# Projecting the two channel tiles of one ring piece back to back in a two-block transformer kernel

## The reference

```python
# block one, last part: 32 experts, each token uses two of one group
a = xb @ w_gate[ex]
u = xb @ w_up[ex]
y = (jax.nn.silu(a) * u) @ w_down[ex]
...
# block two, first part, for 256 context tokens and then for the 256 latent ones
z, xbc, dt_raw, qkv, gate, b_raw, a_raw = jnp.split(h @ w_in, splits, axis=-1)
xbc = jax.nn.silu(conv(xbc, conv_w_ssd) + conv_b_ssd).astype(f32)
qkv = jax.nn.silu(conv(qkv, conv_w_gdn)).astype(f32)
```

## Time and profile before

| What | Before |
|---|---|
| median of 3 runs | 1917.05 us (1910.17 to 1922.61) |
| the profiled execution | 1916.31 us |
| its span in the trace | 1914.6 us |
| TensorE matmul busy | 1723.0 us (90%) |
| TensorE weight load busy | 1214.9 us (63%) |
| VectorE busy | 681.9 us (36%) |
| ScalarE busy | 435.7 us (23%) |
| GpSimd busy | 214.2 us (11%) |
| loaded from memory | 369.98 MB, 194 GB/s over the span |
| mean granted clock of TensorE | 0.947 of full |

### The profile page before, as it was taken

How to read it: one execution, slowest core, us unless ns; L and a number is a source line. 1 busy time by engine, 2 the same in 40 slices (tenths; PEclk the granted TensorE clock), 3 DMA queues, 4 the chain that set the end, 5 groups by cost and what they waited for, 6 DMA issues and landing times.

```text
span 1914.6 us, 25449 instructions
## 1 busy us (share of the span) xinstructions
PE 1723.0 (90%) x10656; PEld 1214.9 (63%) x10656; DVE 681.9 (36%) x1404; ACT 435.7 (23%) x889; POOL 214.2 (11%) x190
## 2 busy tenths in 40 slices
PE   7999999998667888999999799899988998699996
PEld 4558555456444554776777588756878884388842
DVE  3116113235222345332332367765455441400003
ACT  1010453014011113233333131222433430000000
POOL 2000000020000002212222100010424320100000
PEclk9999999989777898999999899999999998799998
DMA  7435336624676979889989824412412123234341
GB/s 250 158 134 173 104 116 225 209 88 172 267 286 247 367 257 377 349 323 418 359 341 417 329 88 161 148 53 89 178 60 74 58 82 125 88 132 148 127 166 43
DMA packets 124296, 372.69 MB, mean 195 GB/s; under 512 B 10524, under 2 KB 26518, under 8 KB 107414
## 3 DMA queue, kind: packets, MB, share of 16 engines
q1 hardware_dynamic: 118245, 361.12, 50.4%
q0 software_dynamic: 1568, 8.39, 1.1%
q10 hardware_dynamic: 4368, 1.54, 0.4%
HBM read 369.98 MB, written 1.05 MB: 194 GB/s over the span
## 4 chain that ended last, share of the span: by engine, by line
PE 74%; DMA 15%; DVE 7%; ACT 1%; issue 1%; SPq 0%; DVEq 0%; ACTq 0%
PE psum L1974 47%; PE psum L569 10%; DMA ring<-in_w_up 7%; DMA ring<-in_w_down 4%; PE psum L1773 4%; PE psum L1968 3%; DMA ring<-in_w_in 3%; PE psum L1795 2%; PE psum L1814 1%; PE psum L1757 1%; PE psum L2091 1%; PE psum L766 1%; DVE area L1201 1%; PE psum L2121 1%; PE psum L555 1%
## 5 line engine op out<-in xcount | busy, mean ns | idle before, releaser
L1974 PE MATMUL psum<-area,ring 128*128 128x256 f32 x1984 | 463.6, 394 | 13.7 <-DMA ring<-in_w_in 12.7
L1974 PE MATMUL psum<-ring,area 128*128 128x512 f32 (+1 forms) x1040 | 452.5, 595 | 7.9 <-DMA ring<-in_w_proj_mem 2.6
L1974 PEld LDWEIGHTS psum<-area,ring 128*128 128x128 f32 x1984 | 389.4, 199 | 81.5 <-DMA ring<-in_w_in 17.6
L1974 PEld LDWEIGHTS psum<-ring,area 128*128 128x128 f32 x1040 | 198.8, 193 | 252.0 <-issue 251.0
L569 PEld LDWEIGHTS psum<-area 128*128 128x128 f32 x2304 | 269.7, 194 | 34.4 <-issue 19.1
L569 PE MATMUL psum<-area 128*128 128x128 f32 x2304 | 280.8, 280 | 10.5 <-DVE area L1178 10.5
L947 ACT ACTIVATE area<-psum 128x512 f32<-128x512 f32 x236 | 138.8, 597 | 243.4 <-PE psum L569 127.4
L2247 ACT ACTIVATE area<-psum 128x512 f32<-128x512 f32 x116 | 66.4, 599 | 458.2 <-PE psum L1974 361.0
L1968 PE MATMUL psum<-const,area 128*128 128x128 f32 x736 | 121.2, 295 | 53.6 <-DVE area L1488 14.8
L1773 PE MATMUL psum<-ring,area 128*32 128x256 f32 x2048 | 132.6, 403 | 23.8 <-DMA ring<-in_w_up 23.8
L1968 PEld LDWEIGHTS psum<-const,area 128*128 128x128 f32 x736 | 90.7, 150 | 99.0 <-issue 23.5
(11 more groups left out here) (304 smaller groups left out, 1341.4 us busy)
## 6 DMA issues: line engine op xcount, KB each, us to landing
ring<-in_w_gate SPq DMA_DIRECT2D x64, 1024.0 KB, 9.6
ring<-in_w_up SPq DMA_DIRECT2D x64, 1024.0 KB, 11.5
ring<-in_w_down SPq DMA_DIRECT2D x64, 1024.0 KB, 11.1
ring<-in_w_in SPq DMA_DIRECT2D x29, 2048.0 KB, 8.4
ring<-in_w_ada SPq DMA_DIRECT2D x12, 2048.0 KB, 8.1
ring<-in_w_in SPq DMA_DIRECT2D x13, 1024.0 KB, 7.8
ring<-in_w_out SPq DMA_DIRECT2D x6, 2048.0 KB, 8.0
ring<-in_w_ffn_gate SPq DMA_DIRECT2D x5, 2048.0 KB, 7.8
```

The source lines that it names most:

```text
L1974: last = nc.tensor.matmul(dst, lhs(k), rhs(k), start=first and k == 0, stop=final and k == count - 1)
```

## The change

The merge in `mixed_schedule` now takes two context phases at once where the first is an even channel tile from 4 to 24, so that the odd tile follows at once and no expert phase stands between them. The list is the same for all engines, so all of them move.

```diff
         while taken < len(context) and given + context[taken][1] / 2 <= total * (i + 1) / (len(experts) - 4):
-            order.append(("context", context[taken][0]))
-            given += context[taken][1]
-            taken += 1
+            paired = context[taken][0] in [f"channel{n}" for n in range(CTX_GAP + 1, 26, 2)]
+            for name, cost in context[taken:taken + 1 + paired]:
+                order.append(("context", name))
+                given += cost
+            taken += 1 + paired
```

## The result

| | Before | After |
|---|---|---|
| median | 1915.0 us | 1868.7 us (1868.0 to 1872.5, 4 runs) |
| ratio | 1 | 0.9759 (0.9722 to 0.9795) |
| profiled execution | 1916.3 us | 1869.3 us |
| its span | 1914.6 us | 1867.6 us |
| matmul busy | 1723.0 us | 1708.2 us |

The change makes the kernel 2.4% faster. The forecast was 1870 us. The 1915.0 us are the median of four runs, the three of above and a fourth.

The account below looks back on a forecast made before the run. Half-read cx slots stalled loads and TensorE in a circle. Step prices put gate_up_a 11 at 668.6 us against 719.7, 51 us less; minus 5 for cold channels leaves 46: 1916 - 46 = 1870 us, range 1858 to 1888.

Parts of the forecast that it names:

- my sum: Step prices added from channel4's start to gate_up_a 11's start: reached at 668.6 us against 719.7, so 51 us less.
- T7: Moment when odd channel 7 is through (Tn likewise for odd channel n): predicted 484.1 us, in the old trace 498.4.
- The circle of a ring held by its reader: Channel stretch: loads wait for a half-read cx slot while TensorE waits for loads; SyncE stands 182.8 us, TensorE 60.1.
- T7 to T9: Channel7 to channel9: load 10.5 us, cold channel 5.8, warm one 3.9; 20.2 us against 29.0 before.
- T9 to T13: Channel9 to channel13: two periods bound by loads, each 7.34 MB at 368 GB/s, 19.9 us.
- The cold surplus: Channels behind a wait may take 6.5 us, not 5.8, in seven periods: 5 us taken from the 51 us gain.
- Does the gain last?: Behind gate_up_a 11, from 719.7 us on: same order and state as before, so nothing of the gain given back.
- rival A: Channel stretch: loads become the bound and take longer, 21.8 us per period; gain 34 us, 1882 us; chance 0.17.
- Rival B: Channel pairs: clock stays low, second channel also takes 6.5 us instead of 3.87; 1891 us; chance 0.08.
- Rival C: Ring slots: pieces come free no earlier in effect, SyncE waits for a gate slot instead; 1916 us; chance 0.04.
- Rival D: Turn behind each pair: pairs clog VectorE, 6.1 us per pair, 67 us for eleven; 1932 us; chance 0.03.
- The activation: Ahead of the transposes of tiles 24 and 25: TensorE's 2.7 us wait goes, counted in the 51 us.

Follow-up runs that it names:

- The late pairs: All eleven pairs made at the place of the odd tile, even tile and its load moved back, against the kernel before: 1867.7 us, ratio 0.9748.
- the version with a piece for each tile and early pairs: Changed kernel's pairs at the even tile's place, plus an own 0.5 MB piece per channel tile from 4 on: 1856.4 us, repeated 1857.4; ratios to kernel before 0.9683, 0.9657.

## Why the prediction was right

The stretch from channel4 to gate_up_a 11 can be laid beside my sum, each as us from the start of channel4 (461.05 after, 460.30 in the sum):

| Point | Sum | After | Before |
|---|---|---|---|
| T7 | 23.8 | 23.0 | 38.2 |
| T9 | 44.0 | 43.8 | 67.2 |
| T13 | 83.8 | 78.7 | 120.0 |
| T17 | 126.6 | 123.2 | 172.8 |
| T21 | 166.4 | 161.3 | 213.2 |
| gate_up_a 11 | 208.3 | 205.5 | 259.4 |

- **What bounds it.** The circle of a ring held by its reader is shown, by the run that only holds the slots (1920.8 us) against the one that frees them (1864.5 us). But the prediction told the circle as a matter of the odd tile standing behind the gate halves. The late pairs (1867.7 us) show that standing behind them is harmless if the piece is read in one go.
- **T7 to T9** was 20.7 us against 20.2. The 5 us for the first load, the 10.5 us to the even tile, and the warm second tile all came as priced; the cold even tile took 6.5 us with its transposes and not 5.8.
- **T9 to T13** was the worst term: 35.0 us (504.80 to 539.79) instead of 2 x 19.9. The two periods took 18.2 and 16.8 us. Two things lay in it. Channel12 was not cold; it took 3.72 us at a granted clock of 1.00, while channel8 took 6.45 us at 0.56. And the loads ran faster than I had allowed: the trace has 393 GB/s for the first of these periods and 404 for the second, where I had taken 368.
- **The cold surplus.** I had taken 5 us off for cold channels at 6.5 us instead of 5.8. The seven cold even tiles in the profile after took 5.2 to 6.7 us with their transposes, 5.9 in the mean, so 0.7 us was to be taken off and not 5. The stretch gained 53.9 us (259.4 less 205.5), not 46.
- **Does the gain last?** I gave nothing back, and the span gained 47.0 us, 6.9 less. 0.75 us was lost ahead of channel4; behind gate_up_a 11 the changed kernel took 1201.1 us against 1194.9, which I had named as a sign of being wrong. In the second profile of the changed kernel this part took 1196.9 us (662.83 to 1859.7) and its stretch 206.2. So the stretch is repeatable, and the part behind it varies by some 4 us from one execution to the next. In the profiles of the versions with a piece for each tile, whose order behind this point is the same, it took 1194.1 to 1201.5 us, so the 6.2 us lie within the scatter; whether a part of them belongs to the change was not settled. The stretch was 7.9 us better than forecast and the rest 6.9 us worse. That the total came within 2 us is in this part luck.
- **The rival A** (21.8 us for a period) did not come: T7 to T23 took 160.5 us (484.08 to 644.54) against the 162.8 of the forecast and 174.4 of A. The single periods ran from 16.8 to 24.0 us, so here too errors of both signs met.
- **Rival B** fell by the timeline: the product of the second tile took 3.62 us in every one of the eleven pairs.
- **Rival C** fell: the waits of SyncE at line 1970 went from 182.8 us in 14 to 120.2 in 16. I had written under 110, so this sign was missed; it was a poor sign, for the reason given with the waits. Of the others, TensorE's waits (29.1 us up to gate_up_a 11) and the DMA share (0.96) came as written, and gate_up_a 11 started at 666.5 us, earlier than the 670 to 675. What speaks against C is the time itself.
- **Rival D** was rightly set low for this kernel. Its price was wrong: with doubled multiply-adds the pairs lost 19.0 us in the stretch and not 36 to 67. TensorE waited for VectorE at a turn behind two of the eleven pairs only, and at most of the others it waits for the load of the down piece anyway.
- **The activation.** Of the 2.7 us ahead of the last transposes that were to go, 1.0 us stayed (L929).
- **The page of the Trainium skill** (DMA: Bandwidth & Descriptors, "Where 436 GB/s comes from") with its limit of about 358 GB/s per core would have given 1873 us. The stretch ran at 372 GB/s over 156.8 us, and 399 GB/s over 25.3 us, so these traces do not show that limit.

## What to carry to other kernels

In a ring of buffers that is filled strictly in order, the price of a buffer is the time from its first use to its last, since a half-read piece stops every load behind the one that wants its slot. That is dear where the loads have nothing else to do meanwhile. Read a piece in one go, or cut it so that each use has its own piece; either was worth 2.4 to 2.8% here, and both together 3.1 to 3.4%. To find such a stall, look for a stretch in which the DMA share is well below one while both the issuing queue and the reader wait, and follow the order of the slots; where the share is already above 0.9, as at the later tiles here, the same edit brings little (0.6%).

## What was not expected of the hardware

The loads of the version with a piece for each tile and early pairs ran at 380 GB/s over 160 us with a DMA share of 1.02 (374 and 1.01 in its second profile). Splitting a 1 MB load with rows of 1 KB into two of 0.5 MB with rows of 512 B cost nothing that shows: the stretch with eleven more loads ran at 373 GB/s at a share of 1.00.

The granted clock was low behind short waits. Channel8, behind waits of 1.27, 1.46 and 1.66 us with work between them, ran at 0.56, so for most of its time at the low level (1.2 GHz), and took 6.45 us; channel12, behind 0.27, 1.60 and 1.35 us, ran at 1.00 (2.4 GHz) and took 3.72 us. The rows of the two stretches:

```profile
494.50:500.80 6.30, 6.27 (x16) 5.06 (x17) 0.00 (x0) 0.00 (x0) 0.00 (x0) 0.56 1.01 419
...
532.20:535.80 3.60, 3.55 (x16) 3.10 (x17) 0.00 (x0) 0.00 (x0) 0.00 (x0) 1.00 1.01 419
```

The second profile of the changed kernel has the same picture: 6.42 us at 0.57 for channel8, behind 1.26, 1.41 and 1.66 us, and 3.72 us at 1.00 for channel12, behind 0.24, 1.51 and 1.50 us. The product itself is the same, so waits of a microsecond or two cost 2.7 us here beyond their length, on the work that followed.
